# Two products of attention moved into the input projection's block, with the value weights' load

## The chip, the cores and the metric

The kernel runs on one core of a Trainium2 chip. The metric is device time in microseconds, the median of the runs. It is written with explicit semaphores: each engine has its own list of instructions, works through it in order, and waits where the list says so. PE is TensorE, DVE is VectorE, ACT is ScalarE, POOL is GpSimd, and SP is SyncE, which here only issues DMAs.

## The reference

One decoder layer on x (1024 tokens, width 1024), in float32:

```python
h     = x @ w_in                       # RWKV columns and MLA columns together
y_rwkv = rwkv7_group(h[..., :RWKV_COLS], ...)
c_q, c_kv, k_pe = split(h[..., RWKV_COLS:], [384, 256, 32])
q = (rms_norm(c_q) @ w_uq).reshape(B, S, 8, 64 + 32)     # "nope" 64, rotary 32 per head
q_nope, q_pe = split(q);  q_pe = rope(q_pe, ang)
kv = (rms_norm(c_kv) @ w_ukv).reshape(B, S, 8, 64 + 64)  # key 64, value 64 per head
k_nope, v = split(kv);  k_pe = rope(k_pe, ang)           # one rotary key for all heads
y_mla = causal softmax attention of [q_nope, q_pe], [k_nope, k_pe], v
mix = concat(y_rwkv, y_mla) @ w_out
x = layer_norm(ALPHA * x + mix)
x = layer_norm(ALPHA * x + relu(x @ w_ffn1)^2 @ w_ffn2)
```

## The kernel before, in words

Every large product is done as three products of rounded parts: high by high, high by low, low by high. The high part is a rounded copy (mostly ScalarE's), the low part is the rest (VectorE's `tensor_tensor` with subtract). So each weight is loaded, copied and subtracted before PE can use it.

The program is a chain of blocks. At the end of a block every engine drains and waits for the others (in the profile these drains and semaphores stand under L231 for the input projection's block). Nothing of the next block starts before.

`input_projection` is the first block. In ten trips of two slabs it makes h (L358), 48 matmuls of 512 columns per slab. Beside the slabs it prepares the latents of attention (`k.lat_hi`, `k.lat_lo`: five tiles, three for the queries, two for keys and values), the rotary angles, and the RWKV group's inputs. PSUM banks 0 to 3 take the slabs, banks 4 to 7 (`Z`, `A_`, `W`, `X`) the small products of the RWKV group, the last of which is masked in the trip before last. At its end SP loads the weights of the rotary and the key products (`later_weights`), ACT and DVE split them (L556, L699), SP stores the masked products (`low_d`, L323), and last comes the store of the last slab (L282), which needs DVE's `mix` of it.

`mla` is the second block, attention. Its first stretch, the front, makes ten products of the latents with weights. In the code they are `("rot", i)`, rotary parts of four heads of queries (18 matmuls); `("nope", i)`, the other part of two heads of queries (18); `("key", i)`, two heads of keys (12); `("value", i)`, values of 256 tokens for all heads (12). `FRONT` is their order on PE. Product n goes to the pair of PSUM banks `PAIRS[n % 3]`, and waits until product n - 3 has been taken out of it:

```python
def left(name):          # what frees a pair
    if kind == "value":   pe.wait_ge(values_taken, i + 1)
    elif kind == "rot":   pe.wait_ge(rot_out, i + 1)
    else:                 pe.wait_ge(staged_lo, STAGE[name][1] + 1)
```

A query or key product is staged: ACT makes `stage_hi` (`stage_product`), DVE makes `stage_lo` (`rest`), SP moves the heads' rows to the tiles `q_hi`, `q_lo`, `k_hi`, `k_lo` of the first three heads or to DRAM for later heads (`stage_leaves`). There are two staging buffers, used in turn by the order `STAGED` = key 0, nope 0, rope 0, rope 1, nope 1, key 1; `stage_free` makes ACT wait until the buffer's last content has landed. A rotary product is copied to `rot_raw` (`rotary_out`, L1215); SP swaps its halves by eight DMAs into `rope_b` (`turn`, L911); DVE's `rotate` (L1283 to L1287) multiplies by `cos4` and, after waiting for the eight DMAs, by `sin4`, and adds; ACT and DVE stage the sum (`stage_rope`, `rest`). Values are copied to `v_all` by ACT (`values_out`, L1221).

Then come the score items of head 0: `s_item(0, qt)` for qt = 7 down to 0, raw scores of 128 queries (L1092), whose row maxima DVE takes (`maxima`, L1301). Some products of the front stand between them. `s_item(0, 7)` waits until key 0, nope 0 and rope 0 have landed in head 0's tiles. `m_item(0)` (L1104) turns the maxima into a row of q, and then head 0's sweep begins (scores transposed, exp, product with values), in which the score items of head 1 are interleaved, and so on for eight heads.

Before the change SP's list of the attention block starts with `w_nope` (three DMAs), `cos4` (four), `w_val` (two), the causal mask, then `turn(0)`; ACT's with the four DMAs of `sin4`; DVE's with the low part of `w_nope` (L1318).

Of the kernel before, what the change touches and what calls it, by code (L numbers as in the profile page):

```python
# [17 lines left out]
ALU = mybir.AluOpType  # L18
ACT = mybir.ActivationFunctionType
# [144 lines left out]

def input_projection(nc, mem, k, t, x, w_in, positions):
# [15 lines left out]
    k.w_key = up_weights(mem, "w_key", 26, 34, [P, KVLT, NH, HD])  # L181
    k.lat_hi = [mem.at(f"latent_hi{c}", kb, [P, S], F32R) for c, kb in enumerate((38, 42, 46, 50, 114))]
# [48 lines left out]
    with ExitStack() as ctx:  # L231
# [14 lines left out]
        normed, latents_hi, latents_lo, up_in, up_hi = sems(  # L246
            nc, ctx, "a_normed", "a_latents_hi", "a_latents_lo", "a_up_in", "a_up_hi")
# [12 lines left out]
        def _(sp):  # L260
# [36 lines left out]
            for n in range(TRIPS):  # L297
# [22 lines left out]
                if 0 < c <= RT:  # L320
                    sp.wait_ge(low_ready, c)
                    for p in range(2):
                        sp.dma_start(matrices(k.low_d)[c - 1, :, p].rearrange("m r j -> r m j"), low[own[p], :, :])\  # L323
                            .then_inc(low_out, 16)
            slab_leaves(1, TRIPS - 1)
# [8 lines left out]
        def _(pe):  # L334
# [78 lines left out]
            for n in range(TRIPS):  # L413
# [19 lines left out]
                else:  # L433
                    slab(n, 1)

        @block.scalar
        def _(act):
# [119 lines left out]
            evict(TRIPS - 1, 1)  # L557

        @block.vector
        def _(dve):  # L560
# [135 lines left out]
            def later_rests():  # L696
                for n, (raw, hi, lo) in enumerate((k.w_rot, k.w_key)):
                    dve.wait_ge(up_hi, n + 1)
                    V.tensor_tensor(lo[:], raw[:], hi[:].bitcast(F32), ALU.subtract)  # L699
# [37 lines left out]
            pair(9, lambda: (mask_low(3), later_rests()), nothing)  # L737
# [27 lines left out]
def mla(nc, mem, k, t):  # L765
# [14 lines left out]
    w_val = up_weights(mem, "w_val", 82, 6, [P, KVLT, NH, HD])  # L780
# [35 lines left out]
    PAIRS = ((2, 3), (4, 5), (6, 7))  # L816
# [16 lines left out]
    FRONT = (("rot", 0), ("key", 0), ("nope", 0), ("value", 0), ("value", 1), ("rot", 1), ("value", 2), ("value", 3),  # L833
             ("nope", 1), ("key", 1))
    PLACE = {name: (n % 3, n // 3) for n, name in enumerate(FRONT)}
    STAGED = (("key", 0), ("nope", 0), ("rope", 0), ("rope", 1), ("nope", 1), ("key", 1)) + tuple(LATE.values())
# [33 lines left out]
    with ExitStack() as ctx:  # L870
# [5 lines left out]
        nope_in, val_in, nope_hi, val_hi, nope_split, val_split = sems(  # L876
            nc, ctx, "b_nope_in", "b_val_in", "b_nope_hi", "b_val_hi", "b_nope_split", "b_val_split")
# [15 lines left out]
        def _(sp):  # L893
# [5 lines left out]
            for n in range(KVLT):  # L899
                heads = t["w_ukv"][:, :, :, HD:P].rearrange("h p c n -> p c h n")  # L900
                sp.dma_start(w_val[0][:, n, :, :], heads[:, n, :, :]).then_inc(val_in, 16)
# [41 lines left out]
            sp.wait_ge(val_split, 1)  # L943
# [51 lines left out]
        def _(pe):  # L995
# [19 lines left out]
            def up(banks, w, i, first, tiles):  # L1015

# [2032 lines left out]
```

## Time and profile before

| | |
|---|---|
| median of 3 runs | 1457.78 us (1457.63 to 1461.37) |
| the profiled execution, its own time | 1463.41 us |
| its span in the profile | 1461.6 us |
| PE busy, mean granted clock | 1389.9 us (95%), 0.971 |
| DVE, ACT, POOL busy | 908.0, 460.8, 460.2 us |
| DMA | 211.80 MB, mean 145 GB/s |
| end of the last slab on PE | 289.2 us |
| start of attention's block | 295.3 us |
| first score item of head 0 | 328.1 us |

Times in the profile count from the span's start. A row of the timeline shows consecutive instructions of one kind on one engine, merged with a count; the bracket at its end is the time that the engine stood idle before it and the engine or DMA that ended this. The windows view gives for a stretch the busy time of each engine with its number of instructions, the granted clock of PE (1.00 is 2.4 GHz, 0.50 is 1.2 GHz), the DMA share and GB/s.

### The profile page before, as it was taken

To read this page: it belongs to the slowest core of one execution; us is meant where nothing else is said; L and a number is where in the kernel's file an instruction comes from. 1 tells how busy PE (TensorE), PEld (TensorE's weight loads), DVE (VectorE), ACT (ScalarE), POOL (GpSimd) and SP (SyncE) were. 2 spreads that over 40 slices of the span, in tenths; PEclk is the share of its full clock that TensorE was granted. 3 is DMA by queue.
4 is the path that set the end of the run, shared out by engine and by line. 5 is a ranking of instruction groups with operands and counts; after the bars stand their busy time and mean duration, and the time that the engine had idled before them with its cause. 6 is when DMAs were issued, how large, how long until landed. Compare 5 with 4: busy or idle time off the path is not lost. (4 is left out here: it accounts for less than half of the span.)

```text
span 1461.6 us, 24895 instructions
## 1 busy us (share of the span) xinstructions
PE 1389.9 (95%) x10592; PEld 1145.2 (78%) x10592; DVE 908.0 (62%) x1030; ACT 460.8 (32%) x640; POOL 460.2 (31%) x282
## 2 busy tenths in 40 slices
PE   6999999978999979998999988999999999999997
PEld 5877888766777669997678876888888888888886
DVE  3547845345465424443558698777777685678887
ACT  2133533122434432332321442221221354434330
POOL 0000221120123210000006668666667254555030
PEclk8999999988999989999899999999999999999999
DMA  5111244486446962111313215444443897655663
GB/s 208 43 46 41 102 144 144 126 187 215 104 133 197 242 174 47 44 43 54 129 59 115 87 58 181 145 146 156 158 159 123 303 320 268 202 186 191 200 194 123
DMA packets 144846, 211.80 MB, mean 145 GB/s; under 512 B 79488, under 2 KB 82176, under 8 KB 144096
## 3 DMA queue, kind: packets, MB, share of 16 engines
q1 hardware_dynamic: 144544, 209.69, 45.3%
q8 instruction: 84, 1.38, 0.4%
q10 hardware_dynamic: 192, 0.52, 0.2%
q14 instruction: 26, 0.21, 0.0%
HBM read 136.18 MB, written 64.29 MB: 137 GB/s over the span
## 5 line engine op out<-in xcount | busy, mean ns | idle before, releaser
L2333 PE MATMUL banks<-stage_b_hi,stage_a_hi 128*128 128x512 f32 x448 | 174.3, 389 | 0.0
L2333 PE MATMUL banks<-stage_b_lo,stage_a_hi 128*128 128x512 f32 x448 | 174.3, 389 | 0.0
L2333 PE MATMUL banks<-stage_b_hi,stage_a_lo 128*128 128x512 f32 x448 | 174.3, 389 | 0.0
L2708 DVE TENSOR_TENSOR stage_a_lo<-stage_a_raw,stage_a_hi 128x1024 fp32r<-128x1024 f32 x56 | 101.7, 1816 | 39.4 <-ACT stage_a_hi L2488 39.4
L358 PE MATMUL banks<-xT_hi,win_hi 128*128 128x512 f32 x320 | 103.5, 405 | 4.7 <-DVE xT_lo L705 4.7
L358 PE MATMUL banks<-xT_lo,win_hi 128*128 128x512 f32 x320 | 100.4, 395 | 0.0
L358 PE MATMUL banks<-xT_hi,win_lo 128*128 128x512 f32 x320 | 100.1, 394 | 0.0
L2333 PEld LDWEIGHTS banks<-stage_b_hi,stage_a_lo 128*128 128x128 f32 x448 | 84.1, 188 | 17.6
L2333 PEld LDWEIGHTS banks<-stage_b_lo,stage_a_hi 128*128 128x128 f32 x448 | 84.1, 188 | 17.4
L2333 PEld LDWEIGHTS banks<-stage_b_hi,stage_a_hi 128*128 128x128 f32 x448 | 84.1, 188 | 17.3
L2488 ACT ACTIVATE stage_a_hi<-stage_a_raw 128x1024 fp32r<-128x1024 f32 x56 | 59.4, 1061 | 116.1 <-DMA stage_b_raw<-in_w_ffn 95.1
L358 PEld LDWEIGHTS banks<-xT_hi,win_hi 128*128 128x128 f32 x320 | 60.7, 192 | 19.2 <-DVE xT_lo L705 4.9
L1140 PE MATMUL banks<-probs,v_all 128*128 128x512 f32 (+3 forms) x192 | 74.9, 504 | 0.7 <-ACT probs L1235 0.7
L1301 DVE TENSOR_REDUCE row_max_parts<-banks 128x1 f32<-128x512 f32 (+1 forms) x96 | 50.1, 552 | 35.1 <-PE banks L1092 23.4
L358 PEld LDWEIGHTS banks<-xT_lo,win_hi 128*128 128x128 f32 x320 | 61.2, 191 | 13.1
L358 PEld LDWEIGHTS banks<-xT_hi,win_lo 128*128 128x128 f32 x320 | 61.2, 191 | 13.1
L1235 ACT ACTIVATE probs<-banks 128x1024 f32<-128x1024 f32 (+3 forms) x64 | 41.5, 650 | 88.7 <-PE banks L1125 51.4
L747 POOL COPY norm_wide<-key_norm 128x1024 f32<-128x1024 f32 x4 | 5.0, 1260 | 185.9 <-DVE cum_tile L666 185.9
L1363 POOL TENSOR_TENSOR att_out<-att_v,att_sum 128x512 f32<-128x512 f32 x7 | 8.9, 1269 | 167.7 <-DVE att_sum L1315 139.9
L2914 POOL TENSOR_TENSOR w_slots<-stage_b_raw,w_slots 128x1024 f32<-128x1024 f32 x16 | 42.8, 2677 | 55.6 <-DMA stage_b_raw<-in_w_ffn 55.6
L2869 POOL TENSOR_TENSOR x<-x,ln_gain 128x1024 f32<-128x1024 f32 x7 | 18.3, 2611 | 116.2 <-DMA ln_bias<-in_ln 113.7
L1805 POOL TENSOR_TENSOR k_undecayed<-hT,undecay 128x256 f32<-128x256 f32 x16 | 11.8, 739 | 134.6 <-ACT undecay L1665 134.6
(401 smaller groups left out, 3712.1 us busy)
## 6 DMA issues: line engine op xcount, KB each, us to landing
stage_b_raw<-in_w_ffn SPq DMA_DIRECT2D x50, 512.0 KB, 4.7
hid_s<-tile_s SPq DMA_DIRECT2D x64, 256.0 KB, 3.9
stage_a_raw<-hid_s SPq DMA_DIRECT2D x32, 512.0 KB, 3.7
w_landed<-in_w_ffn SPq DMA_DIRECT2D x30, 512.0 KB, 5.4
hid_h<-tile_h SPq DMA_DIRECT2D x48, 256.0 KB, 2.0
stage_a_raw<-hid_h SPq DMA_DIRECT2D x24, 512.0 KB, 3.8
win_raw<-in_w_in SPq DMA_DIRECT2D x20, 512.0 KB, 3.7
x_tok<-in_x SPq DMA_DIRECT2D x8, 512.0 KB, 7.1
```

Source lines behind the costliest of these rows:

```text
L358: last = mm(ps[:, 2 * j + b, :], w[j][:, kt, :], r[:, kt, b * HALF:(b + 1) * HALF], start=kt == 0 and i == 0, stop=kt == KT - 1 and i == 2)
L747: G.tensor_copy(out, src).then_inc(wide_done, 1)
L1140: last = mm(ps[:, O[b], lo - b * HALF:HALF], pair[:, 64 * (h % 2):64 * (h % 2) + P], probs[kt % 3][:, lo:(b + 1) * HALF], start=kt == 0, s ...
L1235: A_(probs[kt % 3][:, kt * P:S], flat(T[kt % 2])[:, kt * P:S], ACT.Exp, scale=SCALE)\
L1301: V.reduce_max(tops[:, n, qt:qt + 1], ps[:, b, 0:width], AX_X).then_inc(a_free[b], 1)
L1363: G.tensor_tensor(k.att_out[:], k.att_v[:], k.att_sum[:], ALU.mult).then_inc(y_ready, 1)
L1805: G.tensor_tensor(kd[m % 2][:], hT[:, T_K:T_K + RT, now(m)], undecay[m % 2][:], ALU.mult)\
L2333: last = nc.tensor.matmul(ps[:, bank, :], s[a][:, j, tok], s[b][:, j, :], start=p == 0 and j == 0 and n == 0, stop=p == NP - 1 and j == 1 ...
L2488: A(s["a_hi"][:], s["a_raw"][:], COPY).then_inc(hi2, 1)
L2708: V.tensor_tensor(s["a_lo"][:], s["a_raw"][:], s["a_hi"][:].bitcast(F32), ALU.subtract).then_inc(lo2, 1)
L2869: step.mark(G.tensor_tensor(x1[:, tt, :], x1[:, tt, :], gain1[:], ALU.mult))
L2914: G.tensor_tensor(dst, a, b, ALU.subtract).then_inc(combined, 1)
```

## The change

- The products `rot 0` and `key 0` are issued at the end of the input projection's PE list, behind the last slab, into banks 4, 5 and 6, 7. They wait for the weights' low parts (`up_lo`) and for the last readers of those banks. In attention's block they are no longer issued; `EARLY = 2` and `made_by` leave their waits out.
- The value weights are loaded by SP in the input projection's block, behind the stores of `low_d` and ahead of the store of the last slab; ACT copies them behind its last eviction, DVE makes their rest last. They lie at other addresses.
- `PAIRS` is turned, so that products 0 and 1 of `FRONT` have the banks that the input block wrote.
- `FRONT` becomes rot 0, key 0, value 0, rot 1, value 1, nope 0, value 2, value 3, nope 1, key 1. Eight of them stand before the first score item (seven before), nope 1 behind items 7 and 6, key 1 behind items 5 and 4, then items 3 to 0.
- ACT's list: `rotary_out(0)`, the four DMAs of `sin4`, key 0, value 0, the copy of `w_nope`, value 1, `rotary_out(1)`, nope 0, value 2, rope 0, value 3, rope 1, nope 1, key 1.
- DVE's list: the rest of key 0 and `rotate(0)` come ahead of the low part of `w_nope`.

```diff
@@ -162,6 +162,18 @@
+def up_product(nc, outs, w, i, lat_hi, lat_lo, tiles):
+
+    cut = slice(i * P, (i + 1) * P)
+    for n, c in enumerate(tiles):
+        for m, (ww, r) in enumerate(((w[1], lat_hi), (w[1], lat_lo), (w[2], lat_hi))):
+            lhs = ww[:, n, :, :].rearrange("p h d -> p (h d)")[:, cut]
+            for b, out in enumerate(outs):
+                last = nc.tensor.matmul(out, lhs, r[c][:, b * HALF:(b + 1) * HALF], start=n == 0 and m == 0,
+                                        stop=n == len(tiles) - 1 and m == 2)
+    return last
+
+
 def input_projection(nc, mem, k, t, x, w_in, positions):
@@ -179,6 +191,7 @@
     k.w_key = up_weights(mem, "w_key", 26, 34, [P, KVLT, NH, HD])
+    k.w_val = up_weights(mem, "w_val", 86, 82, [P, KVLT, NH, HD])
     k.lat_hi = [mem.at(f"latent_hi{c}", kb, [P, S], F32R) for c, kb in enumerate((38, 42, 46, 50, 114))]
...
@@ -322,6 +335,11 @@
                             .then_inc(low_out, 16)
+            sp.wait_ge(low_mm, RT)
+            sp.wait_ge(beta_out[1], 16 * RT // 2)
+            heads = t["w_ukv"][:, :, :, HD:P].rearrange("h p c n -> p c h n")
+            for c in range(KVLT):
+                sp.dma_start(k.w_val[0][:, c, :, :], heads[:, c, :, :]).then_inc(val_in, 16)
             slab_leaves(1, TRIPS - 1)
@@ -432,6 +450,15 @@
                     slab(n, 1, 4, key_sums((n - 4,), 0, n + 1))
                 else:
                     slab(n, 1)
+
+            pe.wait_ge(latents_lo, QLT + KVLT)
+            for done, (w, at, tiles) in enumerate(((k.w_rot, Z, range(QLT)), (k.w_key, A_, range(QLT, QLT + KVLT)))):
+                pe.wait_ge(up_lo, done + 1)
+                if at == Z:
+                    pe.wait_ge(low_ready, RT)
+                else:
+                    pe.wait_ge(kk_done, RT)
+                up_product(nc, (ps[:, at, :], ps[:, at + 1, :]), w, 0, k.lat_hi, k.lat_lo, tiles)
         @block.scalar
         def _(act):
@@ -555,6 +582,8 @@
             evict(TRIPS - 1, 1)
+            act.wait_ge(val_in, 16 * KVLT)
+            A(k.w_val[1][:], k.w_val[0][:], ACT.Copy).then_inc(val_hi, 1)
@@ -696,7 +725,12 @@
                     dve.wait_ge(up_hi, n + 1)
-                    V.tensor_tensor(lo[:], raw[:], hi[:].bitcast(F32), ALU.subtract)
+                    V.tensor_tensor(lo[:], raw[:], hi[:].bitcast(F32), ALU.subtract).then_inc(up_lo, 1)
+
+            def value_rest():
+                dve.wait_ge(val_hi, 1)
+                raw, hi, lo = k.w_val
+                V.tensor_tensor(lo[:], raw[:], hi[:].bitcast(F32), ALU.subtract)
@@ -734,7 +768,7 @@
             pair(8, lambda: keys_and_mask(3), lambda: decay_keys(3))
-            pair(9, lambda: (mask_low(3), later_rests()), nothing)
+            pair(9, lambda: (mask_low(3), later_rests()), value_rest)
@@ -777,7 +811,7 @@
     w_nope = up_weights(mem, "w_nope", 106, 197, [P, QLT, NH, HD])
-    w_val = up_weights(mem, "w_val", 82, 6, [P, KVLT, NH, HD])
+    w_val = k.w_val
     solve = mem.at("solve", 82, [P, RT, SB, SB])
@@ -813,7 +847,7 @@
     T = ((2, 3), (4, 5))
-    PAIRS = ((2, 3), (4, 5), (6, 7))
+    PAIRS = ((4, 5), (6, 7), (2, 3))
     flat = lambda pair, rows=slice(0, P): ps[rows, pair[0]:pair[0] + 2, :].rearrange("p b n -> p (b n)")
@@ -830,9 +864,11 @@
-    FRONT = (("rot", 0), ("key", 0), ("nope", 0), ("value", 0), ("value", 1), ("rot", 1), ("value", 2), ("value", 3),
+    FRONT = (("rot", 0), ("key", 0), ("value", 0), ("rot", 1), ("value", 1), ("nope", 0), ("value", 2), ("value", 3),
              ("nope", 1), ("key", 1))
+    EARLY = 2
     PLACE = {name: (n % 3, n // 3) for n, name in enumerate(FRONT)}
+    made_by = lambda name: PLACE[name][1] + (PLACE[name][0] >= EARLY)
     STAGED = (("key", 0), ("nope", 0), ("rope", 0), ("rope", 1), ("nope", 1), ("key", 1)) + tuple(LATE.values())
...
@@ -896,9 +931,6 @@
                 sp.dma_start(cos4[32 * j:32 * j + 32, :], k.trig_in[pe32, :]).then_inc(turns_in, 16)
-            for n in range(KVLT):
-                heads = t["w_ukv"][:, :, :, HD:P].rearrange("h p c n -> p c h n")
-                sp.dma_start(w_val[0][:, n, :, :], heads[:, n, :, :]).then_inc(val_in, 16)
             sp.dma_start(causal[:], t["causal"]).then_inc(causal_in, 16)
@@ -940,7 +972,6 @@
                 sp.dma_start(part, zeros[0:part.shape[0], :]).then_inc(zeros_out, 16)
-            sp.wait_ge(val_split, 1)
             sp.wait_ge(values_taken, RT)
@@ -1012,29 +1043,17 @@
-            def up(banks, w, i, first, tiles):
-
-                cut = slice(i * P, (i + 1) * P)
-                for c in range(tiles):
-                    for n, (ww, r) in enumerate(((w[1], lat_hi), (w[1], lat_lo), (w[2], lat_hi))):
-                        lhs = ww[:, c, :, :].rearrange("p h d -> p (h d)")[:, cut]
-                        for b in range(2):
-                            last = mm(ps[:, banks[b], :], lhs, r[first + c][:, halves[b]],
-                                      start=c == 0 and n == 0, stop=c == tiles - 1 and n == 2)
-                return last
-
             def queries(i, banks):
                 pe.wait_ge(nope_split, 1)
-                return up(banks, w_nope, i, 0, QLT)
+                return up_product(nc, [ps[:, b, :] for b in banks], w_nope, i, lat_hi, lat_lo, range(QLT))
             def rotary(i, banks):
-                return up(banks, k.w_rot, i, 0, QLT)
+                return up_product(nc, [ps[:, b, :] for b in banks], k.w_rot, i, lat_hi, lat_lo, range(QLT))
             def keys_of(i, banks):
-                return up(banks, k.w_key, i, QLT, KVLT)
+                return up_product(nc, [ps[:, b, :] for b in banks], k.w_key, i, lat_hi, lat_lo, range(QLT, QLT + KVLT))
             def values(i, banks):
-                pe.wait_ge(val_split, 1)
                 for b in range(2):
@@ -1163,14 +1182,14 @@
-            for name in FRONT[:7]:
+            for name in FRONT[EARLY:8]:
                 front(name)
...
             pe.wait_ge(consts_set, 1)
-            for n, name in enumerate(FRONT[7:] + (None,)):
-                s_item(0, 7 - 2 * n)
-                s_item(0, 6 - 2 * n)
+            for qts, name in (((7, 6), FRONT[8]), ((5, 4), FRONT[9]), ((3, 2, 1, 0), None)):
+                for qt in qts:
+                    s_item(0, qt)
                 if name:
@@ -1193,7 +1212,8 @@
                 j = stage_free(name)
-                act.wait_ge(made[pair], n + 1)
+                if made_by(name):
+                    act.wait_ge(made[pair], made_by(name))
                 A_(stage_hi[j][:], flat(PAIRS[pair]), ACT.Copy).then_inc(staged_hi, 1)
...
@@ -1248,21 +1269,18 @@
                     last = A_(k.att_v[64 * b:64 * b + 64, :], ps[v_rows, O[b], :], ACT.Copy)
                 last.then_inc(o_read, 1)
+            rotary_out(0)
             for j in range(4):
                 act.dma_start(sin4[32 * j:32 * j + 32, :], k.trig_in[sw32, :]).then_inc(turns_in, 16)
-            rotary_out(0)
+            stage_product(("key", 0))
+            values_out(0)
             act.wait_ge(nope_in, 16 * QLT)
             A_(w_nope[1][:], w_nope[0][:], ACT.Copy).then_inc(nope_hi, 1)
-            stage_product(("key", 0))
-            act.wait_ge(val_in, 16 * KVLT)
-            act.wait_ge(turns_in, 128)
-            A_(w_val[1][:], w_val[0][:], ACT.Copy).then_inc(val_hi, 1)
-            stage_product(("nope", 0))
-            values_out(0)
-            stage_rope(0)
             values_out(1)
             rotary_out(1)
+            stage_product(("nope", 0))
             values_out(2)
+            stage_rope(0)
             values_out(3)
             stage_rope(1)
             stage_product(("nope", 1))
@@ -1314,12 +1332,10 @@
                 dve.wait_ge(o_read, h + 1)
                 V.reciprocal(k.att_sum[:, cut], k.att_sum[:, cut]).then_inc(inverted, 1)
+            rest(("key", 0))
+            rotate(0)
             dve.wait_ge(nope_hi, 1)
             V.tensor_tensor(w_nope[2][:], w_nope[0][:], w_nope[1][:].bitcast(F32), ALU.subtract).then_inc(nope_split, 1)
-            rest(("key", 0))
-            dve.wait_ge(val_hi, 1)
-            V.tensor_tensor(w_val[2][:], w_val[0][:], w_val[1][:].bitcast(F32), ALU.subtract).then_inc(val_split, 1)
-            rotate(0)
             rest(("nope", 0))
             rest(("rope", 0))
             dve.wait_ge(causal_in, 16)
```

New addresses: `w_val` raw and low part share 86 KB, the high part has 82 KB.

## Rows read from the trace of the kernel before

**Rows 1.** PE's timeline, 288 to 349 us: start us, us, engine, line, out<-in, count, [idle before].

```profile
288.56 0.61 PE L358 MATMUL banks<-xT_hi,win_lo 128*128 128x512 f32 x2
295.29 1.19 PE L1022 MATMUL banks<-latent_hi,w_rot_hi 128*128 128x512 f32 x2 [6.12 <-PEq L231]
...
303.80 0.61 PE L1022 MATMUL banks<-latent_hi,w_key_lo 128*128 128x512 f32 x2
306.73 1.22 PE L1022 MATMUL banks<-latent_hi,w_nope_hi 128*128 128x512 f32 x2 [2.32 <-DVE w_nope_lo L1318]
...
328.13 1.19 PE L1092 MATMUL banks<-k_hi,q_hi 96*128 96x512 f32 x2 [3.32 <-DMA rope_d<-stage_lo]
...
330.87 0.73 PE L1042 MATMUL banks<-w_val_hi,latent_hi 128*128 128x512 f32 x1
...
335.05 0.52 PE L1092 MATMUL banks<-k_hi,q_hi 96*128 96x512 f32 x2
...
348.06 1.01 PE L1104 MATMUL banks<-ident_r,neg_row_max_r 128*1 128x128 f32 x8 [2.98 <-DVE neg_row_max_r L1308]
```

**Rows 2.** Windows view, inside the slabs and behind the first stop.

```profile
256.00:274.00 18.00, 18.00 (x81) 14.92 (x80) 6.42 (x6) 2.18 (x2) 5.71 (x2) 1.00 0.43 144
295.25:299.70 4.45, 4.41 (x11) 3.48 (x12) 0.00 (x0) 0.00 (x0) 4.39 (x6) 0.50 0.83 171
```

**Rows 3.** The input block's closing drains: duration ns, first and last start.

```profile
L231 PEldq DRAIN  x1: 4267/4267/4267, 285.0 to 285.0; - x1
...
L231 SPq DRAIN  x1: 63/63/63, 295.0 to 295.0; - x1
```

**Rows 4.** SP's DMA issues from the timeline.

```profile
283.10 2.47 SPq L323 DMA_DIRECT2D low_d<-low_keys  x2
291.67 0.34 SPq L282 DMA_DIRECT2D v_d<-slab  x1
...
297.29 3.93 SPq L898 DMA_DIRECT2D cos<-trig_in  x4
301.26 1.81 SPq L901 DMA_DIRECT2D w_val_raw<-in_w_ukv  x2
303.11 2.46 SPq L902 DMA_DIRECT2D causal<-in_causal  x1
305.61 4.95 SPq L911 DMA_DIRECT2D rope_b<-rot_raw  x8
...
321.35 1.81 SPq L919 DMA_DIRECT2D q_hi<-stage_hi  x3
```

**Rows 5.** VectorE's timeline around attention's first products.

```profile
304.92 1.76 DVE L1318 TENSOR_TENSOR w_nope_lo<-w_nope_raw,w_nope_hi 128x1536 fp32r<-128x1536 f32 x1 [13.27 <-ACT w_nope_hi L1255]
...
312.60 1.23 DVE L1285 TENSOR_TENSOR rope_b<-rope_b,sin 128x1024 f32<-128x1024 f32 x1 [0.40 <-DMA rope_b<-rot_raw]
...
320.05 1.22 DVE L1293 TENSOR_TENSOR stage_lo<-rope_a,stage_hi 128x1024 fp32r<-128x1024 f32 x1 [3.83 <-ACT stage_hi L1207]
...
337.58 1.22 DVE L1293 TENSOR_TENSOR stage_lo<-rope_a,stage_hi 128x1024 fp32r<-128x1024 f32 x1
...
345.69 1.22 DVE L1293 TENSOR_TENSOR stage_lo<-banks,stage_hi 128x1024 fp32r<-128x1024 f32 x1 [1.09 <-ACT stage_hi L1197]
```

**Rows 6.** ScalarE's timeline, same stretch.

```profile
303.39 1.49 ACT L1255 ACTIVATE w_nope_hi<-w_nope_raw 128x1536 fp32r<-128x1536 f32 x1 [0.64 <-DMA w_nope_raw<-in_w_uq]
...
318.96 1.06 ACT L1207 ACTIVATE stage_hi<-rope_a 128x1024 fp32r<-128x1024 f32 x1 [2.54 <-DMA k_lo<-stage_lo]
319.92 1.06 ACT L1221 ACTIVATE v_all<-banks 128x512 f32<-128x512 f32 x2
```

**Rows 7.** DMA view: issues by tile, KB each, median us to landing.

```profile
w_val_raw<-in_w_ukv SPq DMA_DIRECT2D x2, 256.0 KB, 6.4
...
rope_d<-stage_hi SPq DMA_DIRECT2D x1, 512.0 KB, 2.6
rope_d<-stage_lo SPq DMA_DIRECT2D x1, 512.0 KB, 3.6
```

More of the change, by code:

```diff
@@ L245, in input_projection @@
             nc, ctx, "a_keys_squared", "a_keys_summed", "a_keys_rooted", "a_norm_done", "a_rotated", "a_ones_in")
-        normed, latents_hi, latents_lo, up_in, up_hi = sems(
-            nc, ctx, "a_normed", "a_latents_hi", "a_latents_lo", "a_up_in", "a_up_hi")
+        normed, latents_hi, latents_lo, up_in, up_hi, up_lo, val_in, val_hi = sems(
+            nc, ctx, "a_normed", "a_latents_hi", "a_latents_lo", "a_up_in", "a_up_hi", "a_up_lo", "a_val_in", "a_val_hi")
         lora_in, tanh_done, z_mm, a_mm, logw_done, rate_done, key_rate, cum_done = sems(
@@ L875, in mla @@
             "b_zeros_out", "b_turns_in", "b_reloaded")
-        nope_in, val_in, nope_hi, val_hi, nope_split, val_split = sems(
-            nc, ctx, "b_nope_in", "b_val_in", "b_nope_hi", "b_val_hi", "b_nope_split", "b_val_split")
+        nope_in, nope_hi, nope_split = sems(nc, ctx, "b_nope_in", "b_nope_hi", "b_nope_split")
         made = sems(nc, ctx, "b_made0", "b_made1", "b_made2")
@@ L1210, in rotary_out @@
                 pair, n = PLACE[("rot", i)]
-                act.wait_ge(made[pair], n + 1)
+                if made_by(("rot", i)):
+                    act.wait_ge(made[pair], made_by(("rot", i)))
                 if i:
@@ L1218, in values_out @@
                 pair, n = PLACE[("value", i)]
-                act.wait_ge(made[pair], n + 1)
+                act.wait_ge(made[pair], made_by(("value", i)))
                 for b in range(2):
```

## The prediction

> **What bounds the kernel now.** I read the page first: TensorE (PE) is busy 95% of the span at a granted clock of 0.97, so a microsecond counts only if it is one in which PE stands still or runs at half clock. The page's chain of waits starts at 873 us and says nothing of the place that the diff touches. So I went to PE's timeline from the last slab of the input projection to attention's first head [rows 1]. Its brackets are the time that PE stood still: 6.12 us between the last slab and the first rotary product, 2.32 us before the first `nope` product, 3.32 us before the first score item (`s_item`), and a stop before the row-maximum item (`m_item`) at 348.06. That item starts head 0's sweep; from there on the two programs issue the same work in the same order, so what moves 348.06 moves the end. The windows view gives what standing still costs besides: 11 matmul records in 4.45 us at a granted clock of 0.50 (1.2 GHz) after the 6.12 us, against 81 in 18.00 us at 1.00 (2.4 GHz) inside the slabs [rows 2]. The block's end comes from the drains: PE had drained at 285.0 + 4.27 = 289.3, SyncE (SP) only at 295.0, after the last slab's store was issued at 291.67 and had landed [rows 3, 4]. Then I read SP's queue [rows 4], VectorE's [rows 5] and ScalarE's [rows 6] through the same stretch, because all three are reordered.
>
> I call T0 the time at which attention's block begins. Before it is 295.26; the first score item comes at T0 + 32.9 and the m item 19.9 us behind that [rows 1].
>
> **The products that move into the input block.** `rot 0` has 18 matmuls and `key 0` has 12. At 18.00 / 81 = 0.222 us each [rows 2] they end 6.7 us after the last slab's 289.17, at 295.9. Nothing holds them: the low parts of both weights are written before, `low_ready` and `kk_done` are older. Their cover is the wait for the last slab's store, and it is a little too short: PE's drain took 0.1 us past its last matmul, and SP's drain at 295.0 was followed by work at 295.26. So T0 = 295.9 + 0.1 + 0.2 = 296.2, or +0.9 us. The Trainium skill (TensorE: Matmul & The Clock Gate, Back-to-back issue gap) gives about 131 ns for each 512-column matmul in a sustained stream. By that the 30 would fit under the store and the +0.9 would be 0; the trace shows 222 ns in such a stream, so the sum goes by the row.
>
> **The value weights' load.** Two issues of 1.81 us in all leave attention's SP queue and come behind the two `low_d` stores, which end at 285.57 [rows 4]. They end at about 287.4, before the last slab's store at 291.67, so nothing on SP is late for them. From the second issue at about 286.5 with 6.4 us to landing [rows 7] they land at 292.9; ScalarE's copy (1.06) and VectorE's rest (1.22), as for other 128x1024 tiles [rows 5, 6], end at 295.2. That is 0.7 us before PE: no cost, but little room. The Trainium skill (DMA: Bandwidth & Descriptors, Specifications) asks for pieces of 512 bytes or more for the full rate, and these weights move in pieces of 256. The trace agrees: 256 KB of them took 6.4 us, 512 KB of the rotated tile in 4 KB rows 3.6 us [rows 7].
>
> **The new wait.** The new PE order after T0 is `value 0`, `rot 1`, `value 1`, then `nope 0`. The first three are 42 matmuls, 9.3 us. `rot_raw` is copied in the first microsecond. `key 0` is staged behind ScalarE's four sine issues; at the pace of SP's cosine issues (3.93 / 4 = 0.98 us each) its rest ends by T0 + 7.2, and `value 1` would start at T0 + 6.7: at most 0.5 us, taken out of the stop that follows. Then `nope 0` waits for the low part of its weights. Before, VectorE made it first thing, at 304.92, and PE went on at 306.73, 1.81 us later [rows 1, 5]. Now the queue of VectorE has `rotate(0)` ahead of it, and inside `rotate(0)` is the wait for the eight DMAs of `turn(0)`. Everything is queued behind that wait: the low part of `w_nope`, so `nope 0`; and on PE, in order, `value 2` and `value 3` behind `nope 0`.
>
> When does the turned tile land? Call it L, counted from T0. On SP the `w_nope` and cosine issues end at 301.22, T0 + 6.0. Then come the causal mask and `turn(0)`; the value weights' 1.81 us between them are gone. The mask's single issue took 2.46 us, with the value weights ahead of it [rows 4]; the first issue in its new place would be like the value weights' there, 0.6 to 1.2 us. So `turn(0)` starts between T0 + 6.6 and T0 + 8.4 (the full 2.46). From its start (305.61) to VectorE's multiply of the landed tile (312.60) it took 7.0 us [rows 4, 5]. That gives L from 13.6 to 15.4. I take 13.8, near the low bound, as the load on the queue is lower. The lowest bound, if the cosine issues too go at the pace of `turn(0)`'s (4.95 / 8 = 0.62 us each, so 1.5 us less than 3.93): 12.
>
> Then: multiply 1.23, add the same, low part and release of PE 1.81: `nope 0` starts at L + 4.3 = T0 + 18.1 [rows 1, 5]. PE stands still for 18.1 - 9.3 = 8.8 us. Before, both stops of this stretch together were 8.4 us; one is now gone, the other is larger.
>
> **From there to the first score item.** It needs the rotated queries in their sets. ScalarE stages them (`stage_rope(0)`) behind `values_out(2)`, so behind `nope 0` and `value 2`, which are 30 matmuls. After 6.12 us of standing still the 30 of `rot 0` and `key 0` took 303.80 + 0.61 - 295.29 = 9.1 us [rows 1], half clock included. Then `values_out(2)` 1.06, staging to VectorE's rest 1.09 (318.96 to 320.05), rest to SP's first issue 1.30 (320.05 to 321.35), first issue to the score item 6.8 (321.35 to 328.13) [rows 1, 4, 5, 6]. The sum is 19.3, so the item comes at T0 + 18.1 + 19.3 = T0 + 37.4, against T0 + 32.9: +4.5 us. The causal and key constants keep their place behind that rest on VectorE, and the item did not wait for them before (its bracket names the DMA).
>
> **From the score item S to the m item.** `value 3` is gone from between the items, and `nope 1` stands at S + 2.7 in its place. `value 3`'s 12 matmuls took 4.2 us, part at half clock; six more at 0.222 make 5.3 us and put items 5 and 4 at S + 8.0. From item 5 to the rest of `rope 1` it was 2.5 us (335.05 to 337.58), so that rest comes at S + 10.6. Its two stores follow, the second issue at about S + 12.3, landing 3.6 us later [rows 7]: S + 15.9. `key 1`'s staging buffer is free only then; its product is done at S + 12.6. Staging 1.06, and rest to m item 2.4 (345.69 to 348.06) [rows 1, 5]: S + 19.3, against 19.9. The gain is 0.6 us. This stretch was bound by PE and is now bound by this transfer.
>
> **Sum.** +0.9 + 4.5 - 0.6 = +4.8 us. The profiled execution has 1463.41 us, so 1468.2 by its own time. It lies 5.6 us above the median shown, 1457.78; the difference applied to that is 1462.6. A change within 0.3% (4.4 us) is about what a measurement of this kernel can't tell from none.
>
> **Bounds of the sum.** Low: L = 12 (-1.8), the second rope store landing in 2.6 us, as the first did (-1.0): +2.0, 1459.8. High: L = 15.4 (+1.6), no gain in the last stretch (+0.6), and some more half clock, at most the 0.4 x 4.4 us of a second cold start (+1.8): +8.8, 1466.6.
>
> **Rivals.**
> The input block ends late by the value weights. If their issue is held up by 2 us, as the mask's was, they land at 295, VectorE drains at 297.3 and T0 is 297.6: +1.4 more, 1464.0. It decides from a landing after 293.6 on. For it: the short room, and a queue that still holds `low_d`. Against it: the issue stands in a quieter stretch. Chance 0.12.
>
> Longer standing still costs more clock. The 8.8 us ahead of `nope 0`, and about 7 ahead of the first score item (against 3.32), may keep the half clock for longer than the 4.4 us behind 6.12 [rows 2]. Once 3.6 us more of it costs 1.8: 1464.4. Against it: 4.4 us is what the longest stop here shows. Chance 0.12.
>
> Not slower: VectorE's order costs nothing, because the turned tile lands before the weights are split. `w_nope` could be copied at 303.39 (T0 + 8.1), its low part could follow 1.53 us later and PE 1.81 after that: `nope 0` at T0 + 11.4. Then S is T0 + 30.7, and in all it is +0.9 - 2.2 - 0.6 = -1.9 us: 1455.9. It needs L at or under 7.1; the change breaks even at L = 9.0. For it: `rot_raw` is ready at T0 + 1 and not, as before, at T0 + 7.5. Against it: SP issues in order, and T0 + 6.0 plus eight issues of 0.62 us is already 11. Chance 0.1.
>
> Faster by over 0.3%: it would need that, and the m item to be reached more than 2.5 us sooner by the order of the items as well. Nothing in the rows gives it. Chance 0.04.
>
> My forecast has the other 0.62, with its own range of 1459.8 to 1466.6. About 0.4 of that lies within 4.4 us, which is 0.25; with the 0.1 of the third rival it is 0.35 for the same, 0.05 faster, 0.60 slower. The range that leaves out no more than 2 in 10 goes from 1457.0 (part of the third rival) to 1467.5.
>
> **What would show it.** In the profile after: `rot 0` and `key 0` without a stop behind the last slab; T0 near 296.2, with PE's drain the last and VectorE's within 1 us before it; three products to T0 + 9.5; then a stop of 7 to 10 us, put down to `w_nope_lo`, with the multiply of `rope_b` waiting for its DMA just ahead; half clock behind it; first score item near 333.6, `key 1` staged on the landing of `rope_d`, m item near 353. I am wrong if `nope 0` starts before T0 + 13, if the first score item comes before 330, or if a later stop of the 20 us ahead of the sweep shrinks by more than 2 us.

## The result and the profile after

The changed kernel takes 1466.79 us (median of 5, 1465.09 to 1470.46), the kernel before 1458.22 (median of 5 on the same chip). The ratio on record, estimated from the timed runs, is 1.0042, 95% interval 1.0025 to 1.0059: 6.1 us slower, 3.6 to 8.6. The quotient of the two medians, 1.0059, lies at the upper end of this interval.

PE's timeline of the changed kernel, at the places of [rows 1]:

```profile
295.42 0.61 PE L172 MATMUL banks<-latent_hi,w_key_lo 128*128 128x512 f32 x2
296.33 0.47 PE L1061 MATMUL banks<-w_val_hi,latent_hi 128*128 128x512 f32 x1 [0.30 <-PEq L244]
...
315.39 1.19 PE L172 MATMUL banks<-latent_hi,w_nope_hi 128*128 128x512 f32 x2 [9.25 <-DVE w_nope_lo L1338]
...
335.32 1.19 PE L1111 MATMUL banks<-k_hi,q_hi 96*128 96x512 f32 x2 [7.77 <-DMA rope_d<-stage_lo]
...
355.01 1.01 PE L1123 MATMUL banks<-ident_r,neg_row_max_r 128*1 128x128 f32 x8 [4.71 <-DVE neg_row_max_r L1326]
```

The stop of 6.12 us at the block's edge is 0.30 us now. Behind it stand 9.25 us ahead of `nope 0`, where 2.32 stood, and 7.77 ahead of the first score item, where 3.32 stood. The m item comes at 355.01 instead of 348.06.

VectorE's timeline shows what `nope 0` waits for (compare [rows 5]):

```profile
300.86 1.23 DVE L1311 TENSOR_TENSOR stage_lo<-banks,stage_hi 128x1024 fp32r<-128x1024 f32 x1 [7.62 <-ACT stage_hi L1217]
308.50 1.23 DVE L1301 TENSOR_TENSOR rope_a<-rot_raw,cos 128x1024 f32<-128x1024 f32 x1 [6.42 <-DMA cos<-trig_in]
311.09 1.22 DVE L1303 TENSOR_TENSOR rope_b<-rope_b,sin 128x1024 f32<-128x1024 f32 x1 [1.36 <-DMA rope_b<-rot_raw]
312.35 1.22 DVE L1305 TENSOR_TENSOR rope_a<-rope_a,rope_b 128x1024 f32<-128x1024 f32 x1
313.49 1.75 DVE L1338 TENSOR_TENSOR w_nope_lo<-w_nope_raw,w_nope_hi 128x1536 fp32r<-128x1536 f32 x1
```

VectorE stands still for 6.42 us and then 1.36 us inside `rotate(0)`. `rotate` has two waits in the code: its first multiply waits for all eight loads of the cosine and sine tables (`turns_in`), its second for the turned tile. Most of the idle time stands at the first. The low part of `w_nope` has no idle time of its own: it only stands behind. ScalarE had ended the high part at 307.95, 5.5 us before. The rows are ScalarE's copy and then SP's queue (compare [rows 4]):

```profile
306.47 1.48 ACT L1278 ACTIVATE w_nope_hi<-w_nope_raw 128x1536 fp32r<-128x1536 f32 x1 [4.67 <-DMA w_nope_raw<-in_w_uq]
```

```profile
285.77 2.04 SPq L342 DMA_DIRECT2D w_val_raw<-in_w_ukv  x2
291.74 0.34 SPq L295 DMA_DIRECT2D v_d<-slab  x1
296.29 3.03 SPq L931 DMA_DIRECT2D w_nope_raw<-in_w_uq  x3
299.37 3.91 SPq L933 DMA_DIRECT2D cos<-trig_in  x4
303.32 0.84 SPq L934 DMA_DIRECT2D causal<-in_causal  x1
304.20 5.12 SPq L943 DMA_DIRECT2D rope_b<-rot_raw  x8
```

One thing has to be put in order before single executions are compared. The span grew by 3.1 us (1461.6 to 1464.7) and the m item by 7.0. Up to the last product with the values of head 7 the distance stays: 518.7 in the profile of before, 525.8 after. From there to the end of the span the kernel before took 942.9 us in its one profile and the changed kernel 938.9; the other programs below took 937.9 to 942.2 there, with nothing changed in that part. The profile of before has a stop there whose cause the records don't name:

```profile
PE banks L1615 <- issue: 2.7, 1, 2.7
```

That is PE's longest of this kind; in the changed kernel's profile the same kind adds 0.4 us on this line. It accounts for 2.3 of the 4.0 us, and the rest stays open. So this stretch says nothing on the change. Below I compare what lies between two points of one execution: the start of the last slab's last matmul, and the first score item, the m item and attention's last value product. Where the program part is the same, they agree well: from the m item to attention's end the nine programs without extra matmuls there took 170.5 to 171.3 us. Ahead of the score item they agree less: the weights of `w_nope` landed 8.1 us behind the block's start in the profile of before and 8.7 in that of e9, with the same code up to there. Each program has one profile, so a difference of less than 1 us in the table may be chance. The table has them for all runs (from the source view, rounded to 0.1 us), with the ratio of times to the kernel before.

| run | score item | m item | attention's end | ratio (95%) |
|---|---|---|---|---|
| before | 39.3 | 59.3 | 229.9 | |
| changed | 46.5 | 66.2 | 237.0 | 1.0042 (1.0025 to 1.0059) |
| e1 low part first | 40.2 | 59.6 | 230.2 | 1.0015 (1.0003 to 1.0028) |
| e2 before, low part last | 48.3 | 68.0 | 238.8 | 1.0054 (1.0035 to 1.0074) |
| e3 products back | 43.0 | 62.7 | 233.4 | 1.0025 (1.0008 to 1.0042) |
| e4 before, values early | 38.7 | 58.4 | 229.3 | 0.9990 (0.9974 to 1.0007) |
| e5 changed, busy stop | 43.9 | 64.5 | 235.8 | 1.0045 (1.0030 to 1.0061) |
| e6 e1, rope 1's rest first | 40.2 | 59.4 | 230.1 | 1.0000 (0.9987 to 1.0012) |
| e7 e4, busy stops | 35.7 | 55.4 | 223.6 | 0.9967 (0.9952 to 0.9982) |
| e8 before, products early | 39.7 | 59.6 | 230.1 | 1.0016 (1.0006 to 1.0026) |
| e9 before, busy stops | 39.6 | 59.6 | 227.8 | 0.9982 (0.9966 to 0.9998) |
| e10 e1, busy stops | 39.8 | 59.1 | 227.4 | 0.9980 (0.9965 to 0.9994) |

7.1 us at attention's end is 0.49% of the time, inside the interval of the measured ratio. The stretch of one profile and the ratio of the timed runs are not the same measure: for e1 and e8 the ratio gives 2 us more than the stretch, for e7 it gives 1.5 us less of a gain. What causes this is open. I take the stretch for where the time goes and the ratio for how much it is.

### The profile page after: what moved, and what is told of

The parts are those of the page before. It is cut to its first block, busy times and chain, and to the rows that moved or that the text cites. A ratio compares the mean times of both kernels' runs of the same rounds, so it can differ in the third digit from the quotient of the medians.

```text
span 1464.7 us, 24893 instructions
## 1 busy us (share of the span) xinstructions
PE 1387.7 (95%) x10592; PEld 1143.5 (78%) x10592; DVE 907.2 (62%) x1030; ACT 460.9 (31%) x640; POOL 460.9 (31%) x282
## 4 chain that ended last, share of the span: by engine, by line
PE 47%; DVE 4%; issue 1%; ACT 0%; POOL 0%; DVEq 0%
PE banks L2349 21%; PE banks L2229 18%; PE banks L2146 6%; DVE t_lo L2695 1%; DVE w_lo L2562 0%; PE banks L2195 0%; DVE wout_lo L2572 0%; PE banks L2217 0%; PE banks L2321 0%; PE banks L2182 0%; PE banks L2173 0%; PE banks L2165 0%; DVE x1T_lo L2695 0%; POOL tile_s L2911 0%; PE banks L2157 0%
## 5 line engine op out<-in xcount | busy, mean ns | idle before, releaser
L2349 PEld LDWEIGHTS banks<-stage_b_lo,stage_a_hi 128*128 128x128 f32 x448 | 84.1, 188 | 17.6
L2349 PEld LDWEIGHTS banks<-stage_b_hi,stage_a_lo 128*128 128x128 f32 x448 | 84.1, 188 | 17.5
L2504 ACT ACTIVATE stage_a_hi<-stage_a_raw 128x1024 fp32r<-128x1024 f32 x56 | 59.4, 1061 | 115.2 <-DMA stage_b_raw<-in_w_ffn 95.6
L2911 POOL TENSOR_TENSOR tile_s<-tile_h,tile_h 128x512 f32<-128x512 f32 x32 | 45.7, 1446 | 26.2 <-DVE tile_h L2709 17.2
```

Source lines behind the costliest of these rows:

```text
L2349: last = nc.tensor.matmul(ps[:, bank, :], s[a][:, j, tok], s[b][:, j, :], start=p == 0 and j == 0 and n == 0, stop=p == NP - 1 and j == 1 ...
L2504: A(s["a_hi"][:], s["a_raw"][:], COPY).then_inc(hi2, 1)
L2911: G.tensor_tensor(dst, a, b, op).then_inc(sums_h, 1)
```

## The experiments

**e1: the low part of `w_nope` ahead of `rotate(0)`, in the changed kernel.**

```diff
             rest(("key", 0))
-            rotate(0)
             dve.wait_ge(nope_hi, 1)
             V.tensor_tensor(w_nope[2][:], ...)
+            rotate(0)
```

> The changed kernel with one edit: on VectorE the low part of w_nope stands ahead of rotate(0) again. My theory (nope 0 waits because its low part is queued behind the wait for the turned tile): nope 0 starts near 310 instead of 315.4, the first score item near 329 instead of 335.3, the m item near 349 instead of 355.0; about 6 us less than the changed kernel, within 0.2% of the kernel before (ratio 1.0005). Rival 1 (the rotation and SP's queue bind the first score item whatever VectorE's order): the item moves by less than 2 us, ratio above 1.003. Rival 2 (the extra time is the later start of the block and the longer half clock): the same, ratio above 1.003.

PE's timeline:

```profile
310.46 1.08 PE L172 MATMUL banks<-latent_hi,w_nope_hi 128*128 128x512 f32 x2 [3.84 <-DVE w_nope_lo L1337]
...
329.61 1.19 PE L1111 MATMUL banks<-k_hi,q_hi 96*128 96x512 f32 x2 [7.75 <-DMA rope_d<-stage_lo]
```

The stop fell from 9.25 to 3.84 us, and 6.8 of the 7.1 us at attention's end are gone. Both rivals said that the score item would move by less than 2 us; it moved by 6.3. By the stretch, the two lines of VectorE's order carry nearly the whole loss. By the timed runs they carry most of it: the ratio falls from 1.0042 to 1.0015, and its interval leaves 0.4 to 4.1 us to the rest of the change.

**e2: the same order in the kernel before, nothing else of the change.** VectorE: rest of key 0, low part of `w_val`, `rotate(0)`, low part of `w_nope`.

> The kernel before with one edit: on VectorE the low part of w_nope goes behind rotate(0); nothing else of the change. My theory: nope 0 starts near 316.8 instead of 306.7, the first score item near 336 instead of 328.1, 7 to 8 us slower than before, ratio 1.005. Rival (the loss comes from the products moved to the input block and from the order of the products): under 2 us slower, ratio under 1.0015.

```profile
315.76 1.22 PE L1022 MATMUL banks<-latent_hi,w_nope_hi 128*128 128x512 f32 x2 [13.47 <-DVE w_nope_lo L1322]
```

+9.0 us to the score item, +8.9 at attention's end, ratio 1.0054. With the last slab at 287.3, 1.5 us sooner than in the profile of before, `nope 0` would stand at 317.3 on that profile's scale (316.8 expected). The order is a cause by itself.

**e3: `rot 0` and `key 0` issued in attention's block again.** The loop behind the last slab is taken out, and `EARLY = 0`.

> The changed kernel with rot 0 and key 0 issued in attention's block again, as its first two products; early value load and all other orders kept. My theory (in this order their 6.8 us lie ahead of a stop that ends by VectorE anyway, so moving them gives nothing and costs T0 its 1 us): block starts near 295.3, nope 0 near 314.5 to 316, time 1 us less to 1 us more than the changed kernel, ratio to before 1.0035 to 1.005. Rival (moving them saves their own time and the loss would be larger without it): 5 us or more slower than the changed kernel, ratio above 1.0075.

```profile
294.90 1.19 PE L172 MATMUL banks<-latent_hi,w_rot_hi 128*128 128x512 f32 x2 [6.06 <-PEq L244]
314.05 0.70 PE L172 MATMUL banks<-latent_hi,w_nope_hi 128*128 128x512 f32 x2 [0.44 <-DVE w_nope_lo L1329]
331.53 1.19 PE L1102 MATMUL banks<-k_hi,q_hi 96*128 96x512 f32 x2 [7.69 <-DMA rope_d<-stage_lo]
```

3.6 us faster than the changed kernel up to attention's end, where I had expected -1 to +1. The rival, that moving the products saves their time, is further off still. `nope 0` starts 19.15 us behind the block's start (314.05 - 294.90), as in the changed kernel (315.39 - 296.33 = 19.06): VectorE's order sets it in both. But PE came to it with a stop of 0.44 us instead of 9.25, and `nope 0` to the score item takes 17.5 us instead of 19.9. The windows view, changed kernel from 315.3, this one from 314.05:

```profile
315.30:320.50 5.20, 5.11 (x12) 4.08 (x13) 0.00 (x0) 0.00 (x0) 0.00 (x0) 0.51 0.00 0
```

```profile
314.05:324.00 9.95, 9.78 (x42) 7.78 (x42) 2.00 (x2) 4.79 (x8) 0.00 (x0) 1.00 0.21 51
```

12 matmuls in 5.2 us at a granted clock of 0.51, against 42 in 9.95 us at 1.00. So moving the 30 matmuls of the two products ahead of the block cost twice in this order: 1.0 us by which the block begins later, and 2.4 us because the gap that they left was standing still, with half clock behind it. By the timed runs, 1.0025 against 1.0042, the two together are 2.5 us, and the intervals of the two ratios overlap.

**e4: the value weights' load in the input block, alone, in the kernel before.** ScalarE's copy and VectorE's rest go with it.

> The kernel before with the value weights' load, copy and low part moved into the input block alone; attention's order and PE's products as before. My theory (before, the first score item hangs on turn(0), the landing of key 0's rows behind it, and the staging of rope 0, and the two loads delay SP by 1.8 to 2.5 us there): turn(0) starts near 303, stage_rope(0) near 316.5 instead of 319.0, first score item near 325.7, 2 to 2.5 us faster than before, ratio 0.9984. Rival (this chain isn't what binds, or the input block ends later by the load): no change or slower.

```profile
299.60 0.58 SPq L911 DMA_DIRECT2D causal<-in_causal  x1
300.94 4.93 SPq L920 DMA_DIRECT2D rope_b<-rot_raw  x8
```

`turn(0)` starts 7.5 us behind the block's start (300.94 - 293.46) instead of 10.3, as expected, but the score item gains only 0.6 us and attention's end 0.6, where 2 to 2.5 were expected. The ratio can't be told from 1. The chain had a second strand: `stage_rope(0)` stands behind `values_out(0)` on ScalarE, that is behind `nope 0` and `value 0` on PE, and this strand came later than before:

```profile
315.66 1.09 ACT L1228 ACTIVATE v_all<-banks 128x512 f32<-128x512 f32 x2 [1.69 <-PE banks L1049]
316.45 1.77 SPq L928 DMA_DIRECT2D q_lo<-stage_lo  x2
316.63 1.06 ACT L1214 ACTIVATE stage_hi<-rope_a 128x1024 fp32r<-128x1024 f32 x1
```

At its start, 316.63, the staging has no idle bracket: it follows `values_out(0)` and not a landing. `values_out(0)` ended 29.4 us behind the last slab here, and 27.6 in the profile of before. `nope 0` had started 0.7 us later behind the last slab, as its weights landed later, and stayed at half clock for 5.3 us (to 311.3) instead of 2.7:

```profile
305.90:309.50 3.60, 3.52 (x8) 2.81 (x9) 3.57 (x5) 0.00 (x0) 0.00 (x0) 0.50 0.62 121
309.50:311.00 1.50, 1.50 (x5) 1.14 (x4) 1.09 (x1) 0.00 (x0) 0.00 (x0) 0.50 0.98 229
```

**e5: PE kept busy in the changed kernel's stop.** The extra matmuls of this and the later runs are of this form; their results are not read.

```diff
+            def busy(count, bank):
+                for _ in range(count):
+                    mm(ps[:, bank, :], <a tile of w_key_hi>, lat_hi[0][:, 0:HALF], start=True, stop=True)
             def queries(i, banks):
+                if i == 0:
+                    busy(38, A[0])
                 pe.wait_ge(nope_split, 1)
```

> The changed kernel with 38 extra matmuls of 512 columns (8.4 us at 0.222 us each) into an unused bank between value 1 and nope 0; their results are not read. The stop ahead of nope 0 and its end stay, PE is only busy in it. Theory of the half clock (2.4 us of what the changed kernel loses is that nope 0 and value 2 run at half clock behind the long stop, as the run with the products moved back suggests: 17.5 us from nope 0 to the first score item, against 19.9): here 17.5 us too, the m item 2.4 us earlier, ratio to before near 1.0025. Rival (the run with the products back gained by something else, T0 or the transfers): no change, 19.9 us and 1.004; and if nope 0 starts later by the extra work, slower.

```profile
304.71 8.78 PE L1048 MATMUL banks<-latent_hi,w_key_hi 128*128 128x512 f32 x38
313.95 0.74 PE L172 MATMUL banks<-latent_hi,w_nope_hi 128*128 128x512 f32 x2 [0.46 <-DVE w_nope_lo L1344]
331.50 1.19 PE L1117 MATMUL banks<-k_hi,q_hi 96*128 96x512 f32 x2 [7.69 <-DMA rope_d<-stage_lo]
```

`nope 0` to the score item is 17.55 us, as in e3, so the 2.4 us are the clock's. The whole is not as expected: score item to m item takes 20.6 us instead of 19.7, because behind the next stop PE stayed at half clock for 7.5 us (to 339) instead of 5.6, with `nope 1` in it. 1.2 us are left at attention's end, and the ratio, 1.0045, shows none. The timed runs leave this one undecided.

**e6: e1 with the rest of `rope 1` ahead of the maxima of items 5 and 4.**

> The run with the low part first, with one more edit: VectorE makes the rest of rope 1 ahead of the maxima of score items 5 and 4. Theory (from the first score item to the m item the new order is bound by the landing of rope 1's second store, which frees the buffer of key 1): the store goes out 2 us earlier, key 1 is staged 2 us earlier, and first score item to m item takes 17.4 us instead of 19.4; 2 us less than that run, ratio to before 0.9995 to 1.0005. Rival (bound by PE's products or by VectorE's maxima): no gain, or 1 us more as the maxima come later.

The gain at the m item is 0.2 us, not 2. `key 1` no longer waits for the store:

```profile
340.38 0.66 PE L1111 MATMUL banks<-k_hi,q_hi 96*128 96x512 f32 x2 [1.73 <-DVE row_max_parts L1319]
...
342.81 1.05 PE L172 MATMUL banks<-latent_hi,w_key_hi 128*128 128x512 f32 x2
```

```profile
345.64 1.02 ACT L1217 ACTIVATE stage_hi<-banks 128x1024 fp32r<-128x1024 f32 x1 [6.26 <-PE banks L172]
```

The store was binding, and was relieved. But item 4 now waited 1.73 us for its bank instead of 0.60, `key 1` followed at half clock (1.05 us for two matmuls instead of 0.62), and its product ended when the store had landed before. One wait took the place of the other.

**e7: e4 with busy stops** (14 matmuls ahead of `nope 0`, 12 ahead of the m item, 3 behind it). In e7, e9 and e10 PE also waits until the values are taken out before the matmuls ahead of the m item.

> The kernel before with the early load of the value weights alone, and extra matmuls whose results are not read: 14 ahead of nope 0, 12 ahead of the m item, 3 behind it, so that PE stays busy through three short stops. Theory of the half clock: nope 0 and the first transposed scores of head 0 run at full clock; 1 us less to the first score item, about 2 us less behind the m item, ratio to before near 0.997. Rival (the stops are too short for the clock to matter, or the extra matmuls hold up what waits behind them): same as that load alone, 0.999, or slower.

```profile
303.34 3.34 PE L1036 MATMUL banks<-latent_hi,w_key_hi 128*128 128x512 f32 x14
323.89 0.69 PE L1105 MATMUL banks<-k_hi,q_hi 96*128 96x512 f32 x2 [0.90 <-DMA rope_d<-stage_lo]
...
340.41 2.99 PE L1036 MATMUL banks<-latent_hi,w_key_hi 128*128 128x512 f32 x12
343.56 0.65 PE L1117 MATMUL banks<-ident_r,neg_row_max_r 128*1 128x128 f32 x8 [0.16 <-DVE neg_row_max_r L1321]
```

3.0 us less than e4 to the score item (1 expected) and another 2.7 us less from the m item to attention's end (2 expected). `stage_rope(0)` again follows `values_out(0)`, which now ended 26.4 us behind the last slab instead of 29.4:

```profile
314.48 1.06 ACT L1223 ACTIVATE stage_hi<-rope_a 128x1024 fp32r<-128x1024 f32 x1
```

Ratio 0.9967: faster than both kernels.

**e8: `rot 0` and `key 0` in the input block, alone, in the kernel before.** `PAIRS` is turned with them.

> The kernel before with rot 0 and key 0 issued in the input block, and nothing else of the change (PAIRS turned for their banks; load of the value weights and all orders as before). Theory (the block begins 1 us later, SP still reaches turn(0) only 10.4 us behind it, and nope 0 still waits for its weights, now behind a longer stop with more half clock): first score item 1 to 2 us later than before, ratio 1.0005 to 1.0015. Rival (the products were on the path and their 6.8 us are saved): 4 us or more faster, ratio below 0.9975.

```profile
306.50 4.94 SPq L934 DMA_DIRECT2D rope_b<-rot_raw  x8
308.19 1.22 PE L1045 MATMUL banks<-latent_hi,w_nope_hi 128*128 128x512 f32 x2 [12.34 <-DVE w_nope_lo L1343]
```

+0.4 us to the score item, +0.2 at attention's end; by the ratio, 1.0016, it is 0.9 to 3.8 us. The products now fill the stop of 6.12 us, and the time that they took in attention is standing still, with the 2.32 us one stop of 12.34. The 6.8 us of products were off the path: `nope 0` waited for its weights as before, which landed 8.8 us behind the block's start (8.1 before), and `turn(0)` stood 10.4 us behind it in SP's queue.

**e9: the kernel before with busy stops alone** (9, 12 and 3 matmuls).

> The kernel before with extra matmuls alone, whose results are not read: 9 ahead of nope 0, 12 ahead of the m item, 3 behind it. No part of the change. Theory (the gain of the run with both comes nearly all from the clock, since the early value load alone gave 0.6 us up to attention's end): 4 to 5 us less than before, ratio 0.997 to 0.998. Rival (the gain needs the early value load, as it frees SP and the clock then only keeps it): 0.999 or above.

Nothing up to the m item (59.6 against 59.3), 2.4 us behind it, 2.1 at the end: about half of what I expected. Ahead of the score item `nope 0` ran at full clock, but `stage_rope(0)` waited for the landing of key 0's rows, as in the kernel before [rows 6]:

```profile
319.24 1.06 ACT L1216 ACTIVATE stage_hi<-rope_a 128x1024 fp32r<-128x1024 f32 x1 [2.39 <-DMA k_lo<-stage_lo]
```

Early values and busy stops gave 0.6 and 2.1 us alone and 6.3 us together. The 2.4 us behind the m item are in both e9 and e7 and simply add. The rest is ahead of the m item: 0.9 us gained by e4, 0.3 lost by e9, 3.9 gained by e7. `stage_rope(0)` has two strands there, the landing behind SP's queue and `values_out(0)` behind PE. In the kernel before, the landing released it 30.2 us behind the last slab, and `values_out(0)` had ended at 27.6. e4 took the landing away, but the other strand moved to 29.4; e9 took the half clock away (27.2), but the landing stayed at 29.6; e7 did both and had 26.4.

**e10: e1 with busy stops** (14, 30 ahead of the score item, 19, 3).

> The run with the low part first (changed kernel, w_nope's low part ahead of rotate(0)) with extra matmuls whose results are not read: 14 ahead of nope 0, 30 ahead of the first score item, 19 ahead of the m item and 3 behind it. Theory (with VectorE's order mended the changed kernel is level with the one before, and its three stops cost half clock behind each): nope 0 to the first score item 17.5 us instead of 19.2, full clock through the score items, about 2 us less behind the m item; 4 to 5 us less than the run with the low part first, ratio to before 0.998. Rival (transfers bind from stage to stage, so only the stretch behind the m item gains): ratio 1.000, and not below.

```profile
311.56 0.74 PE L172 MATMUL banks<-latent_hi,w_nope_hi 128*128 128x512 f32 x2 [1.37 <-DVE w_nope_lo L1347]
...
329.46 0.70 PE L1117 MATMUL banks<-k_hi,q_hi 96*128 96x512 f32 x2 [0.69 <-DMA rope_d<-stage_lo]
...
348.79 0.64 PE L1129 MATMUL banks<-ident_r,neg_row_max_r 128*1 128x128 f32 x8 [0.28 <-DVE neg_row_max_r L1336]
```

2.8 us less than e1 at attention's end, 2.3 of them behind the m item. `nope 0` to the score item took 17.9 us, but `nope 0` started 0.7 us later behind the last slab, as its weights landed 11.0 us behind the block's start instead of 10.2. The full clock through the score items brought nothing to the m item (19.3 us against 19.4), since from there the path is rope 1's store. Ratio 0.9980, where 0.998 was expected, though by the one term and not by the others. The new order with VectorE's list mended stays 3.8 us behind e7.

## Why the prediction was right

The drains of the changed kernel's first block:

```profile
L244 PEldq DRAIN  x1: 4240/4240/4240, 291.8 to 291.8; - x1
L244 DVEq DRAIN  x1: 1240/1240/1240, 292.0 to 292.0; - x1
L244 SPq DRAIN  x1: 7/7/7, 295.0 to 295.0; - x1
```

Direction, mechanism and place were as predicted; each term of the sum came out somewhat on the slow side.

- **T0.** +0.9 forecast, 296.30 - 295.26 = +1.0 measured, by PE's drain (291.8 + 4.24 = 296.0, compare [rows 3]): VectorE's `w_val` rest ended at 293.2 (292.01 + 1.23), so the rival of late value weights did not come up. They landed before 291, sooner than my 292.9; VectorE was done 2.8 us before PE and not, as forecast, within 1 us.
- **The new wait.** It is where it was put, and its releaser is the low part of `w_nope` behind `rotate(0)` (e1, e2). L is 311.09 - 296.30 = 14.8 instead of 13.8. The step that was mis-sized is the start of `turn(0)`: the mask's issue fell to 0.84 us as argued, but the three `w_nope` issues took 3.03 us instead of the 1.98 that I carried over, so `turn(0)` started at T0 + 7.9, not T0 + 6.8. `nope 0` is at T0 + 19.1 (18.1 forecast). The prediction, and the description of `rotate` ahead of it, left out the first wait in `rotate(0)`, the one for the tables. It ended at 308.50, T0 + 12.2, so early enough that the turned tile still came last, by 1.4 us.
- **`nope 0` to score item.** 19.9 us, 19.3 forecast. The item is at T0 + 39.0, not 37.4.
- **Score item to m item.** 19.7 us, 19.3 forecast. The binding transfer was named rightly: `key 1`'s staging waits for rope 1's second store (e6 takes that wait away). Its gain is 0.2 us instead of 0.6.

```profile
351.58 1.02 ACT L1217 ACTIVATE stage_hi<-banks 128x1024 fp32r<-128x1024 f32 x1 [6.74 <-DMA rope_d<-stage_lo]
```

- **Sum.** 1.0 + 6.1 - 0.2 = +6.9 at the m item, 4.8 forecast. The ratio's interval, +3.6 to +8.6 us, holds both.

What the prediction did not see is the part of the half clock. It stood inside the 9.1 us taken over for 30 matmuls, and in a rival as an extra for a longer stop. Little of such an extra showed: about 5.1 us at half clock behind `nope 0`'s stop against 4.4 behind the 6.12 us, and about 5.6 behind the first score item's 7.77 us, the same as behind the 3.32 us before. But the change also made the stop: with the two products left in attention's block PE would have been at work until 0.44 us before `nope 0` (e3). So the products, which I booked at +0.9 us for the later block, cost 3.6 in this order by the stretch. Alone they cost 0.2 us by the stretch (e8), and 0.9 to 3.8 by the ratio.

The rival on the other side, that VectorE's order costs nothing, asked for the turned tile at T0 + 9.0 or sooner. SP's eight issues alone ended at T0 + 13.0. The tables rule it out as well: with the turned tile there in time, the two multiplies, the sum and the low part would still follow the tables' T0 + 12.2. By this profile's rows that is an estimate of T0 + 17.6 for `nope 0` (308.50, then 1.14 for the first multiply as at 338.89 to 340.03 in VectorE's timeline, and 4.30 from the second multiply to PE), and the rival needs T0 + 13.3 to break even. So fewer issues for `turn(0)` or another queue, which no run tried, could have gained about 1.4 us here. Its row for the weights did not hold either: they landed at T0 + 10.2 instead of T0 + 8.1, and e1, with the order mended, has `nope 0` at T0 + 13.6 and not T0 + 11.4. Why they landed later with the same three loads first in SP's queue is open.

## What to carry to other kernels

Before an instruction is put behind another on the same engine, ask what the other waits for, not how long it takes: here 3.7 us of multiplies and add stood in front, with 7.8 us of waiting inside, most of it in a wait that the prediction did not list. Products moved forward out of a stretch that ends on something else leave a stop behind, and the stop can cost by the half clock of what follows (2.4 us here, in e3 and e5). If the path splits into strands that end close to each other (30.2 and 27.6 us here), a repair of one shows little until the other is repaired too: up to the m item 0.9 us gained, 0.3 lost, and together 3.9 gained. Matmuls whose results nobody reads are a cheap probe of what the clock takes, and here a gain.

## What was new of the hardware

- The clock fell behind much shorter stops than the 6.12 us of [rows 2]. In e6 PE stood still for 1.73 us, worked for 1.5 us at full clock and then ran at half clock:

```profile
340.90:341.90 1.00, 1.00 (x6) 0.87 (x6) 0.98 (x3) 0.00 (x0) 0.00 (x0) 1.00 1.00 401
341.90:345.50 3.60, 3.60 (x10) 2.77 (x10) 1.04 (x1) 0.00 (x0) 0.00 (x0) 0.53 0.74 221
```

  The stop alone does not decide it: in e10 a stop of 1.37 us stood between 14 extra matmuls and `nope 0`, and the granted clock stayed at 1.00 behind it (311.5 to 318.0).
- The same three issues of `w_nope` took SP 1.98 us in the profile of before, 2.52 in e1, 3.03 in the changed kernel and 3.22 in e6, and `turn(0)` started 7.2, 7.9 and 7.8 us behind the block's start in the last three. An issue's duration in a busy queue is no constant to be carried over.
- The last slab's last matmul started between 287.3 and 289.9 in the twelve profiles; in before, e2 and e9, whose code is the same up to there, at 288.8, 287.3 and 289.6. So times are compared from a common point inside each execution.
